# Expert rows by fp32 products with kept pick tables instead of an indirect gather and transposes

## The reference, cut to what matters

```
logits = (x @ router_w) + router_b
top_vals, top_idx = top_k(logits, 2);  top_w = softmax(top_vals)
gate = sum(one_hot(top_idx, 8) * top_w)
for e in range(8):
    out = out + gate[..., e:e+1] * ((silu(x @ w1[e]) * (x @ w3[e])) @ w2[e])
```

## Time and profile before

| what | value |
|---|---|
| median of 3 runs | 1484.82 us (1482.34 to 1489.27) |
| the profiled execution | 1488.29 us |
| its span, first to last instruction | 1486.5 us |
| PE busy, share of the span | 94% |
| DVE, ACT, POOL busy | 68%, 54%, 5% |
| mean granted TensorE clock | 0.961 of full speed |
| DMA moved | 317.98 MB, mean 214 GB/s |
| chain that ended last, by engine | PE 85%, DVE 10%, ACT 3% |

### The profile page before, as it was taken

How to read it: one execution, slowest core, us unless ns; L and a number is a source line. 1 busy time by engine, 2 the same in 40 slices (tenths; PEclk the granted TensorE clock), 3 DMA queues, 4 the chain that set the end, 5 groups by cost and what they waited for, 6 DMA issues and landing times.

```text
span 1486.5 us, 20384 instructions
## 1 busy us (share of the span) xinstructions
PE 1398.1 (94%) x8149; PEld 1230.9 (83%) x8149; DVE 1017.0 (68%) x1018; ACT 803.6 (54%) x810; POOL 72.6 (5%) x93
## 2 busy tenths in 40 slices
PE   6986899999999988999999999889999999999995
PEld 6985799999888867999988888678888788888884
DVE  5596545456556686545565566768888788888886
ACT  5653354544565343454435644426776677767673
POOL 1000000000100000000000000008000000000000
PEclk9996899999999988999999999979999999999998
DMA  9522465665535434666746354448999999999991
GB/s 281 180 94 57 116 192 174 184 201 182 179 114 177 128 117 133 203 181 186 213 156 203 97 176 122 146 156 305 371 359 345 353 333 341 351 358 362 356 331 45
DMA packets 240898, 317.98 MB, mean 214 GB/s; under 512 B 10544, under 2 KB 145840, under 8 KB 240688
## 3 DMA queue, kind: packets, MB, share of 16 engines
q1 hardware_dynamic: 236096, 300.52, 60.9%
q0 software_dynamic: 4720, 16.32, 3.9%
HBM read 314.70 MB, written 2.10 MB: 213 GB/s over the span
## 4 chain that ended last, share of the span: by engine, by line
PE 85%; DVE 10%; ACT 3%; issue 1%; DMA 1%; SPq 0%; DVEq 0%; ACTq 0%
PE ps L1658 26%; PE ps L1659 25%; PE ps L1660 25%; PE ps L2002 1%; DVE w_lo L1001 1%; PE ps L2021 1%; PE ps L2220 1%; PE ps L1985 1%; DMA raw<-in_w_in_dram 1%; DVE x L1045 1%; DVE x L1044 1%; PE ps L2178 1%; DVE small L1019 1%; PE ps L1692 1%; PE ps L2179 1%
## 5 line engine op out<-in xcount | busy, mean ns | idle before, releaser
L1001 DVE TENSOR_TENSOR w_lo<-raw,w_hi 128x2048 fp32r<-128x2048 f32 x130 | 297.2, 2291 | 197.9 <-ACT w_hi L589 175.9
L589 ACT ACTIVATE w_hi<-raw 128x2048 fp32r<-128x2048 f32 x106 | 201.7, 1907 | 131.0 <-PE ps L1660 119.9
L1658 PE MATMUL ps<-xt_hi,w_hi 128*128 128x256 f32 x912 | 262.2, 287 | 1.8 <-DVE xt_lo L1091 1.1
L1659 PE MATMUL ps<-xt_lo,w_hi 128*128 128x256 f32 x912 | 261.0, 286 | 0.0
L1660 PE MATMUL ps<-xt_hi,w_lo 128*128 128x256 f32 x912 | 261.0, 286 | 0.0
L1658 PEld LDWEIGHTS ps<-xt_hi,w_hi 128*128 128x128 f32 x912 | 178.4, 196 | 5.2 <-issue 2.7
L1659 PEld LDWEIGHTS ps<-xt_lo,w_hi 128*128 128x128 f32 x912 | 178.4, 196 | 0.9
L1660 PEld LDWEIGHTS ps<-xt_hi,w_lo 128*128 128x128 f32 x912 | 178.0, 195 | 0.0
L1534 DVE TENSOR_TENSOR w_lo<-raw,w_hi 128x2048 fp32r<-128x2048 f32 (+1 forms) x65 | 143.5, 2215 | 31.0 <-ACT w_hi L909 30.8
L1658 PE MATMUL ps<-w_hi,xt_hi 128*128 128x512 f32 (+2 forms) x432 | 157.3, 364 | 4.6 <-DVE xt_lo L1015 3.1
L1660 PE MATMUL ps<-w_hi,xt_lo 128*128 128x512 f32 (+2 forms) x432 | 153.9, 356 | 0.0
(11 more groups left out here) (398 smaller groups left out, 2624.4 us busy)
## 6 DMA issues: line engine op xcount, KB each, us to landing
raw<-in_moe_w_dram SPq DMA_DIRECT2D x144, 512.0 KB, 5.6
raw<-in_w_in_dram SPq DMA_DIRECT2D x99, 512.0 KB, 4.7
scr<-in_moe_w_dram SPq DMA_DIRECT2D x90, 512.0 KB, 7.5
raw<-in_ffn_w_dram SPq DMA_DIRECT2D x66, 512.0 KB, 4.6
scr<-in_moe_w_dram SPq DMA_DIRECT2D x54, 384.0 KB, 5.0
raw<-in_w_gate_dram SPq DMA_DIRECT2D x22, 512.0 KB, 4.0
raw<-in_w_up_dram SPq DMA_DIRECT2D x22, 512.0 KB, 5.2
raw<-in_w_down_dram SPq DMA_DIRECT2D x22, 512.0 KB, 4.3
```

What stands on the lines that cost most here:

```text
L589: A_(w_hi[:, slot, :], raw[:, slot, :], ACT.Copy).then_inc(hi_ready, 1)
L1001: TTo(w_lo[:, slot, :], raw[:, slot, :], w_hi[:, slot, :].bitcast(F32), ALU.subtract).then_inc(lo_ready, 1)
L1658: MM(dst, a_hi, b_hi, start=start, stop=False)
L1659: MM(dst, a_hi, b_lo, start=False, stop=False)
```

## The change

The rows of experts 1 to 7 come by the same fp32 products as those of expert 0. Their place in PE's order is that of the transposes which they replace, into the same PSUM bank and with the same semaphore. For this the pick tables have to stay until expert 7's rows are made, so they move from the scratch area into the memory of `xt_hi`, which holds turned tokens up to the router and is free after it. The landing places of the gather, for the passes 8 to 10 that are left with it, move to `xt_lo`, and the third to the front of `xt_hi`, for which POOL waits until the products of expert 7 are done. POOL works out the left-over tokens first, and then issues the gathers of passes 8, 9 and 10.

```diff
+        xt_at = nc.sbuf_base + (-nc.sbuf_base) % 32
         xt_hi = sb("xt_hi", [P, KT, T], F32R)
...
-        x_rows = [flat(xt_hi)[:, 0:D].bitcast(F32), flat(xt_hi)[:, D:2 * D].bitcast(F32), flat(xt_lo)[:, 0:D].bitcast(F32)]
-        pick = area(10240, TT, EXPERTS, P)
+        x_rows = [flat(xt_lo)[:, 0:D].bitcast(F32), flat(xt_lo)[:, D:2 * D].bitcast(F32), flat(xt_hi)[:, 0:D].bitcast(F32)]
+        pick = over("pick", xt_at, 0, TT * EXPERTS * P, F32)[:, :].rearrange("p (t e s) -> p t e s", t=TT, e=EXPERTS)
...
         def rows_place(e):
-            return (2, 1) if e == EXPERTS + 2 else (e % 2, (e + 1) // 2)
+            return e - EXPERTS, 1
...
-            for e in range(1, EXPERTS + SPILLS):
-                if e == 2:
-                    find_spills()
-                    sum_spills()
-                    pick_spills()
-                pool.wait_ge(ev("slots_ready"), 1 if e == 1 else 2 if e < EXPERTS else 3)
-                if 2 <= e < EXPERTS + 2:
-                    pool.wait_ge(x_turned, 2 * (e - 1))
+            pool.wait_ge(ev("slots_ready"), 1)
+            find_spills()
+            sum_spills()
+            pick_spills()
+            for e in range(EXPERTS, EXPERTS + SPILLS):
+                pool.wait_ge(ev("slots_ready"), 3)
+                if e == EXPERTS + 2:
+                    pool.wait_ge(x_turned, 2 * EXPERTS)
                 place, _ = rows_place(e)
                 pool.indirect_dma_start(x_rows[place], None, x_dram, bass.IndirectOffsetOnAxis(slot_token[:, e:e + 1], 0)) \
                     .then_inc(rows_gathered[place], 16)
...
             def turn_gathered(e, half, bank):
+                if e < EXPERTS:
+                    for k in range(4):
+                        d = half * 512 + k * P
+                        for t in range(TT):
+                            last = MM(ps[:, bank, k * P:(k + 1) * P], x[:, t, d:d + P], pick[:, t, e, :], start=t == 0, stop=t == 1)
+                    last.then_inc(x_turned, 1)
+                    return
                 place, count = rows_place(e)
                 pe.wait_ge(rows_gathered[place], 16 * count)
                 for k in range(4):
```

## The result

The kernel after takes 1500.18 us in the median of 4 runs (1496.97 to 1503.68), the kernel before 1484.53 us (1482.34 to 1489.27): a ratio of 1.0102 with a 95% interval of 1.0068 to 1.0135. It is slower by 15.7 us, where 18.9 were forecast; the time lies in the stated range.

The account below looks back on a forecast made before the run. PE, full in the expert part, was taken as the bound: 3.57 - 0.87 = 2.70 us an expert, times 7 = 18.9 us, nothing elsewhere. 1484.82 + 18.9 = 1503.7 us, range 1497 to 1511 us.

Parts of the forecast that it names:

- PE as the bound, and all of it on the path: Expert part: PE has no free time (54.92 of 55 us), so whatever is added to its list adds to the time.
- Rival B: Weight ring, experts 1 to 7: transfers are the bound, dropping 3.7 MB gives 10.4 us back, time 1474 us; chance 0.03.
- The price of a product, 0.223 us: Experts 1 to 7: 16 fp32 products each, at attention's full-clock rate, 3.57 us an expert.
- rival C: New products: part is cheap, as with 64 still columns; sum near 6 us, time 1491 us; chance 0.05.
- The price of a transpose, 0.109 us: Experts 1 to 7: eight transposes each go, four take 0.44 us on the chain, saving 0.87 us an expert.
- The clock: New blocks run at clock 1.00; expert 3's fall to half clock may come or not, 0 to -1.5 us.
- Rival A: Behind each of 14 product blocks the clock falls to 1.2 GHz, 1.5 us each, 21 us more, 1525 us; chance 0.06.
- Unless it falls into the 0.1 us of idle in 55: PE in the expert part: added work costs time except what fits its idle, put at 0.1 us in 55.
- take_rows, POOL's order, the memory: Row splits on ACT and DVE behind the products, POOL's earlier left-over tokens, moved tables: each claimed to cost 0 us.

## Why the prediction was right, and which term was off

**PE as the bound, and all of it on the path.** Right. With PE at 54.92 of 55 us a second helping of products cost 3.57 us for 3.57 us. The full DMA engines did not decide: kept gathers changed nothing (52.80 against 52.81 us). Rival B is out.

**The price of a product, 0.223 us.** Right: 1.78 us a block, 0.2225 us a product, from attention's rows. The half-clock rate of expert 0 would have given 6.7 us an expert, and the cheap products of rival C 0.9 us; C is out too. Why the price is what it is, the prediction did not say; the run with half of the columns shows that it is not the moving columns, and leaves the rest open.

**The price of a transpose, 0.109 us.** Right, since a difference of 2.68 us came out where the wait is in neither (both kernels with the early gate product). The four-times rule of the Trainium skill, "TensorE: Matmul & The Clock Gate", section "Terms", would have made it 3.12 us, as the prediction worked out, and does not hold for these transposes.

**The clock.** Right: 1.00 through all fourteen blocks and the 3 us behind each, even doubled ones. Rival A is out. In expert 3 the fall was there in the kernel after as in that before, so it gave no difference between them.

**"Unless it falls into the 0.1 us of idle in 55".** This is the term that was mis-sized: the waiting of PE into which the added products could fall was 0.32 us an expert. The prediction took it as next to nothing, and held against rival B that the products next to the transposes step by an even 0.24 us. That is so behind the first group of transposes and not behind the second, where the earlier trace rows has 0.09 us "issue" and the next product on the chain took 0.47 us. Together these are 0.32 us. The table of waits from which the earlier trace rows was read also had it, as weight loads that wait 2.7 us in nine places for "issue". The windows hid it, because the record of the last transpose lasts longer than its step and covers most of the gap; the weight loads showed it as 0.30 us. The longer products of the second half run while DVE finishes `gate_up(2)`, and so 0.32 of their 1.34 us cost nothing. Seven times 0.32 is 2.2 us: 18.9 - 2.2 = 16.7, which is what the stretch shows. Against the medians' 15.7 us (10.1 to 20.0 by the interval) both 16.7 and 18.9 are possible. The two runs that leave PE's steps as in the kernel after were 1501.78 - 1485.10 = 16.7 us (gathers kept) and 1502.05 - 1485.51 = 16.5 us (half of the moving columns) above the kernel before, which fits 16.7 better; but it is the distances within a trace that tell the two apart. Of the 3.5 us by which the median of 1500.18 us lies under the likeliest 1503.7, the hidden wait accounts for 2.2 us; the other 1.3 us lie within the scatter of such medians.

**take_rows, POOL's order, the memory.** Right at 0, by the run with the memory alone and by that with the gathers kept.

## What to carry to other kernels

Where one engine is full, a change to its list is priced by step times of the same shape at the same clock elsewhere in the trace, and here that price held to 0.01 us a block, whatever it freed on engines that wait. To find what may still be hidden, don't read only the busy share: look at the weight loads too, and behind every short group at the first instruction that takes twice its usual time, and ask which semaphore that instruction waits for even if the profile says "issue". A wait that longer work covers is better taken away at its source: here one line moved on DVE gave 0.2 to 0.3%, where the products that covered it cost 1%.

## What the runs showed of the hardware

- At full clock an fp32 product with 128 still columns steps at 0.10 to 0.11 us a record, two records each, whether 2 columns (twelve records in 1.23 us), 64 (16 in 1.73 us) or 128 (16 in 1.78 us) move through it. What fewer columns save in the block comes back in the first product behind it (0.29 us in place of 0.23 with 64), so they bought nothing.
- A transpose of 128 x 128 fp32 has one such record (four in 0.44 us), and costs half of a product (16 records, eight products, in 1.78 us) and not a quarter.
- Twelve fp32 records with two moving columns behind 0.9 us of idle were followed by half clock in expert 3 of some executions (the kernel before) and not of others (the run with the first half by products: 54.23 us for expert 3, where 51.77 + 3.97 = 55.7 us would have shown the same fall).
- Seven gathers of 0.52 MB beside the weight stream, with a DMA share of 0.97 and 0.98 in place of 0.94 and 0.96, moved the time of an expert by no more than 0.01 us (52.80 against 52.81). The weights were loaded ahead of their use: their queue waited for free places.
